# Joint attention stage: single key banks between other work on TensorE, that work one step later, a ring of three PSUM banks

## What is computed

```python
def _diff_combine(s, lam):
    p = jax.nn.softmax(s, axis=-1)
    B, _, Q, K = p.shape
    p = p.reshape(B, H_C, 2, Q, K)
    return p[:, :, 0] - lam * p[:, :, 1]

# prompt, for each block of 128 queries
s = jnp.einsum('bqhd,bkhd->bhqk', qi, k).astype(F32) * HD_C ** -0.5
s = jnp.where((kpos[None, :] <= qpos[:, None])[None, None], s, -jnp.inf)
a = _diff_combine(s, lam)
return jnp.einsum('bhqk,bkhe->bqhe', a, vf)

# samples
kp = cache_k[o][page_table].reshape(Bs, past, 2 * H_C, HD_C)
vp = cache_v[o][page_table].reshape(Bs, past, H_C, 2 * HD_C)
```

## Time and profile before

| | |
|---|---|
| median of three executions | 3101.52 us (3096.23 to 3102.09) |
| the profiled execution | 3103.92 us, its span 3101.8 us |
| busy share of the span: PE, DVE, ACT | 86%, 43%, 26% |
| the attention stage | from about 2013 to 2952 us of the span |
| DMA of the whole span | 535.76 MB |

### The profile page before, as it was taken

One profiled execution on the slowest core, in us unless ns is written; L12 is line 12 of the kernel. 1 busy time (PEld: TensorE's weight loads), 2 busy tenths in 40 slices (PEclk: granted clock), 3 DMA queues, 4 the chain that ended last, 5 costly groups with the idle time before them and its releaser, 6 DMA issues. The chain is left out here.

```text
span 3101.8 us, 45074 instructions
## 1 busy us (share of the span) xinstructions
PE 2677.2 (86%) x16187; PEld 1953.2 (63%) x16187; DVE 1345.8 (43%) x2285; ACT 797.2 (26%) x1981; POOL 392.1 (13%) x232
## 2 busy tenths in 40 slices
PE   4999999999929995899599999588888888888858
PEld 3988889888817774444277777455555555555546
DVE  3456553332234665122223433155555555555533
ACT  3122111111113331011111111144444444444421
POOL 3123322233000000000231311000000000000000
PEclk9999999999958998999899999799999999999979
DMA  3233321332146896521232331688898897897642
GB/s 108 79 95 98 100 79 58 112 105 80 55 108 185 274 287 193 197 82 44 66 96 90 112 95 53 197 303 278 318 337 283 312 336 276 322 341 278 242 144 93
DMA packets 323449, 535.76 MB, mean 173 GB/s; under 512 B 28525, under 2 KB 231810, under 8 KB 320042
## 3 DMA queue, kind: packets, MB, share of 16 engines
q1 hardware_dynamic: 320482, 524.66, 50.5%
q10 hardware_dynamic: 2792, 8.82, 0.8%
HBM read 432.06 MB, written 101.22 MB: 172 GB/s over the span
## 5 line engine op out<-in xcount | busy, mean ns | idle before, releaser
L2230 PE MATMUL at_ring<-ident,at_kp 128*128 128x128 f32 x2048 | 304.3, 287 | 126.6 <-DVE at_kT L2452 69.9
L2230 PEld LDWEIGHTS at_ring<-ident,at_kp 128*128 128x128 f32 x2048 | 230.8, 145 | 199.8 <-issue 145.2
L2452 DVE COPY at_kT<-at_ring 128x512 f32<-128x512 f32 x256 | 177.1, 692 | 182.1 <-PE at_ring L2230 168.4
L497 PE MATMUL p_col<-h_hi,p_wqk 128*128 128x352 f32 x768 | 248.7, 324 | 3.2 <-DVEq L675 3.2
L1884 PE MATMUL p_gm<-p_whl,h_hi 128*128 128x512 f32 (+1 forms) x576 | 229.9, 399 | 21.9 <-POOLq L1946 21.9
L499 PE MATMUL p_col<-h_hi,p_wqk 128*128 128x352 f32 x768 | 247.0, 322 | 0.0
L498 PE MATMUL p_col<-h_lo,p_wqk 128*128 128x352 f32 x768 | 246.9, 321 | 0.0
L1611 PE MATMUL oa_out<-oa_w,oa_yT 128*128 128x512 f32 x512 | 225.7, 598 | 9.0 <-ACT oa_yT L1667 5.4
L526 PE MATMUL p_row<-p_wvz,h_hi 128*128 128x512 f32 (+1 forms) x576 | 228.9, 397 | 3.6 <-ACT p_vst L600 3.6
L528 PE MATMUL p_row<-p_wvz,h_lo 128*128 128x512 f32 (+1 forms) x576 | 227.7, 395 | 0.0
L1886 PE MATMUL p_gm<-p_whl,h_lo 128*128 128x512 f32 (+1 forms) x576 | 227.7, 395 | 0.0
(11 more groups left out here) (341 smaller groups left out, 4431.4 us busy)
## 6 DMA issues: line engine op xcount, KB each, us to landing
at_kp<-in_cache_k SPq DMA_DIRECT2D x256, 512.0 KB, 4.7
at_vp<-in_cache_v SPq DMA_DIRECT2D x256, 512.0 KB, 5.7
p_wst<-in_w_in_a SPq DMA_DIRECT2D x64, 512.0 KB, 4.2
s_qk<-p_res SPq DMA_DIRECT2D x32, 528.0 KB, 2.8
mx_qk<-s_qk SPq DMA_DIRECT2D x16, 1024.0 KB, 10.6
p_wst<-in_w_in_c SPq DMA_DIRECT2D x64, 256.0 KB
s_v<-p_vst SPq DMA_DIRECT2D x64, 128.0 KB, 2.8
s_g<-p_gst SPq DMA_DIRECT2D x64, 128.0 KB, 2.7
```

The source lines that it names most:

```text
L497: pe.matmul(out[:, r, 0:TN], wx[:, 0, k, :], h_hi[:, k, at], start=k == 0, stop=False)
L2230: last = pe.transpose(bank("key", n, 2 * k + f)[:, h * PAGE:(h + 1) * PAGE], kp[:, n % 2, k, (4 * f + h) * P:(4 * f + h + 1) * P], c.ident[:])
L2452: dve.tensor_copy(kT[:, n % 2, 4:8, k * PAGE:(k + 1) * PAGE], bank("key", n, 2 * k + 1)[:].rearrange("p (h t) -> p h t", h=4)).then_inc(dv ...
```

## The change

Every piece stays, with the same shapes; three things are altered, all in `attend`.

1. The ring has three banks, and a fill waits for the use three places earlier. The bank `ov` is gone: the page values go through the ring as a ninth kind of use, taken by `add_page`.
2. PE's step is cut finer. `turn_keys` fills one bank, `page_scores` comes in two halves of four matmuls, and single key banks stand between the other pieces. The turned weights and the page scores of step s move to step s + 1, the rows to s + 2, the page values to s + 3, the pick one step later too; so the loop has one pass more (`LAST`).
3. ACT, DVE and SP follow. DVE's maximum is taken for each half apart (one more `tensor_reduce` and `tensor_scalar` a step, the elements the same), and ACT's two exponentials stand apart. SP issues the first key page of s + 2, then four value pages, then the other three key pages, and the store and the loads of a head in iteration 3 in place of 2.

The diff, cut to its core:

```diff
+    RING = 3
...
-        ring = [st.ps(f"ring{i}", [P, 512]) for i in range(2)]
+        ring = [st.ps(f"ring{i}", [P, 512]) for i in range(RING)]
         sc = st.ps("sc", [P, 2, T])
         ssc = st.ps("ssc", [P, 512])
-        ov = st.ps("ov", [P, 512])
...
-        LAST = NG + 3
+        LAST = NG + 4
...
+        def keys_at(s):
+            return s < NG
+
+        def weights_at(s):
+            return 1 <= s <= NG
+
+        def rows_at(s):
+            return 2 <= s <= NG + 1
+
+        def values_at(s):
+            return 3 <= s <= NG + 2
+
+        def pick_at(s):
+            return (s - 4) // NGB if s >= 4 and (s - 4) % NGB == NGB - 1 else None
+
         for s_ in range(LAST):
-            for k in range(GP):
-                if s_ < NG:
-                    use("key", s_, 2 * k, "act")
-                    use("key", s_, 2 * k + 1, "dve")
-                if k == 1 and 1 <= s_ <= NG:
+            for f in range(2 * GP):
+                if keys_at(s_):
+                    use("key", s_, f, ("act", "dve")[f % 2])
+                if f == 1 and values_at(s_):
+                    use("val", s_ - 3, 0, "dve")
+                if f == 2 and weights_at(s_):
+                    for i in range((tiles(s_ - 1) + 3) // 4):
+                        use("wgt", s_ - 1, i, ("act", "dve")[i])
+                if f == 4 and rows_at(s_):
+                    use("row", s_ - 2, 0, "act")
+                if f == 5 and weights_at(s_):
                     use("out", s_ - 1, 0, "act")
-                if k == 2 and 1 <= s_ <= NG:
-                    use("row", s_ - 1, 0, "act")
-            if s_ < NG:
-                for f in range((tiles(s_) + 3) // 4):
-                    use("wgt", s_, f, ("act", "dve")[f])
-            if s_ >= 2 and s_ - 2 < NG and (s_ - 1) % NGB == 0:
-                use("pick", (s_ - 1) // NGB - 1, 0, "act")
+            if pick_at(s_) is not None:
+                use("pick", pick_at(s_), 0, "act")
...
         def bank(kind, n, i):
-            return ring[fills[kind, n, i] % 2]
+            return ring[fills[kind, n, i] % RING]
 
         def wait_bank(pe, kind, n, i):
 
             u = fills[kind, n, i]
-            if u >= 2:
-                eng, count = uses[u - 2]
+            if u >= RING:
+                eng, count = uses[u - RING]
...
-                def keys(n):
-                    for k in range(GP):
-                        if n >= 2:
-                            sp.wait_ge(filled, fills["key", n - 2, 2 * k + 1] + 1)
-                        page(g["cache_k"], kp, k_loaded, n, k)
-
-                def values(n):
-                    for k in range(GP):
-                        if n >= 2:
-                            sp.wait_ge(v_used, GP * (n - 2) + k + 1)
-                        page(g["cache_v"], vp, v_loaded, n, k)
+                def key(n, k):
+                    if n >= 2:
+                        wait_fill(sp, "key", n - 2, 2 * k + 1)
+                    page(g["cache_k"], kp, k_loaded, n, k)
+
+                def value(n, k):
+                    if n >= 2 and k < GP - 1:
+                        sp.wait_ge(v_used, (GP - 1) * (n - 2) + k + 1)
+                    elif n >= 2:
+                        wait_fill(sp, "val", n - 2, 0)
+                    page(g["cache_v"], vp, v_loaded, n, k)
...
+                for s in range(NG + 1):
+                    if s + 2 < NG:
+                        key(s + 2, 0)
+                    if s >= 3:
+                        for k in range(GP):
+                            value(s - 1, k)
+                    if s + 2 < NG:
+                        for k in range(1, GP):
+                            key(s + 2, k)
+                    if s % NB == 3 and s >= NB:
+                        store(s // NB - 1)
+                        if s // NB + 1 < HC:
+                            head(s // NB + 1)
...
+                def turn_keys(n, f):
+                    k = f // 2
+                    if f % 2 == 0:
+                        pe.wait_ge(k_loaded[n % 2 * GP + k], 16 * (n // 2 + 1))
+                    wait_bank(pe, "key", n, f)
+                    for h in range(4):
+                        tile = (4 * (f % 2) + h) * P
+                        last = pe.transpose(bank("key", n, f)[:, h * PAGE:(h + 1) * PAGE], kp[:, n % 2, k, tile:tile + P], c.ident[:])
+                    last.then_inc(filled, 1)
...
+                    wait_bank(pe, "val", n, 0)
...
+                        last.then_inc(v_used if k < GP - 1 else filled, 1)
+
+                def page_scores(n, i):
+                    if i == 0:
+                        pe.wait_ge(act_took, took("key", n, 2 * GP - 2))
+                        pe.wait_ge(dve_took, took("key", n, 2 * GP - 1))
+                        if n >= 1:
+                            pe.wait_ge(p_ready, n)
+                    for j in range(JC):
+                        last = pe.matmul(ssc[32 * j:32 * j + 32, :], qz[:, n // NGB, j, i, :], kT[:, n % 2, j + JC * i, :],
+                                         start=i == 0, stop=i == 1)
+                    if i == 1:
+                        last.then_inc(s_ready, 1)
...
-                    if s < NG:
-                        turn_keys(s, 0)
-                    if 2 <= s <= NG + 1:
-                        page_values(s - 2)
-                    if s < NG:
-                        turn_keys(s, 1)
-                    if 1 <= s <= NG:
-                        sum_values(s - 1)
-                    if s < NG:
-                        turn_keys(s, 2)
-                    if 1 <= s <= NG:
-                        turn_rows(s - 1)
-                    if s < NG:
-                        turn_keys(s, 3)
-                        if s + 1 < NG:
-                            scores(s + 1)
-                        page_scores(s)
-                        turn_weights(s)
-                    if picks(s) is not None:
-                        pick(picks(s))
+                    for f in range(2 * GP):
+                        if keys_at(s):
+                            turn_keys(s, f)
+                        if f == 1 and values_at(s):
+                            page_values(s - 3)
+                        if f == 2 and weights_at(s):
+                            turn_weights(s - 1)
+                        if f == 3 and weights_at(s):
+                            page_scores(s - 1, 0)
+                        if f == 4 and weights_at(s):
+                            page_scores(s - 1, 1)
+                        if f == 4 and rows_at(s):
+                            turn_rows(s - 2)
+                        if f == 5 and weights_at(s):
+                            sum_values(s - 1)
+                    if s + 1 < NG:
+                        scores(s + 1)
+                    if pick_at(s) is not None:
+                        pick(pick_at(s))
...
-                def exps(s):
+                def exps(s, m):
                     n = tiles(s) * P
-                    act.wait_ge(max_ready, s + 1)
-                    for m in range(2):
-                        last = act.activation(pr[:, s % 2, m, 0:n], sc[:, m, 0:n], ACT.Exp, bias=o_mx[:, s % 2, m:m + 1], scale=SC,
-                                              accum_out=o_den[:, s % 2, m:m + 1])
-                    last.then_inc(sc_taken, 1)
+                    act.wait_ge(max_ready, 2 * s + m + 1)
+                    last = act.activation(pr[:, s % 2, m, 0:n], sc[:, m, 0:n], ACT.Exp, bias=o_mx[:, s % 2, m:m + 1], scale=SC,
+                                          accum_out=o_den[:, s % 2, m:m + 1])
+                    if m == 1:
+                        last.then_inc(sc_taken, 1)
...
+                    if rows_at(s):
+                        page_exps(s - 2)
+                    if keys_at(s):
+                        take_keys(s, 0)
+                        take_keys(s, 1)
+                    if weights_at(s):
                         take_weights(s - 1)
-                    if picks(s - 1) is not None:
-                        take_pick(picks(s - 1))
-                    if s < NG:
-                        take_keys(s, 0)
-                    if 1 <= s <= NG:
-                        page_exps(s - 1)
-                    if s < NG:
-                        take_keys(s, 1)
-                        exps(s)
-                    if 1 <= s <= NG:
+                    if keys_at(s):
+                        exps(s, 0)
+                        take_keys(s, 2)
+                    if rows_at(s):
+                        take_rows(s - 2)
+                    if keys_at(s):
+                        exps(s, 1)
+                    if weights_at(s):
...
-                    dve.wait_ge(v_used, GP * (n + 1))
+                    wait_fill(dve, "val", n, 0)
...
+                def maximum(s, m):
+                    top = o_mx[:, s % 2, m:m + 1]
+                    ch.link(dve.tensor_reduce(top, sc[:, m, 0:tiles(s) * P], AX_X, ALU.max))
```

(60 more changed lines are left out.)

51 lines of the change are left out of this document (10 added, 41 removed).

## The result

The changed kernel takes 2935.2 us (median of four, 2928.86 to 2948.84), the kernel before 3101.81 us in the same session: a ratio of 0.947, 95% interval 0.9435 to 0.951. The forecast was 2948, so the gain is 167 us where 154 were expected. The profiled execution took 2939.19 us, its span is 2937.1.

A forecast was written before the change was run, and what follows sets the result against it. PE was taken as the bound, idle in waits for free ring banks. Pace 88, stalls 5, changes of piece 2 and clock 1 make 96 us a head, 768 against 922.4: gain 154, median 2948 us, range 2915 to 3020.

The forecast's parts named there:

- PE's pace: In the attention stage, PE's unchanged matmuls and transposes take 88 us a head at full clock.
- The named stalls: PE's waits left at four places in the new order: 4.4 us, with 1 us of restarts about 5 a head.
- Tile count 8 into 1: PE waits 0.8 us for the page values' bank, behind ACT's rows and exponential and DVE's difference and key bank 7.
- Tile count 3: DVE's finish delays PE 1.2 us at the weights and 1.15 at the page values' bank: 2.35 us.
- The small ones at tile counts 2, 4, 7 and 8: Page values' bank 0.2 to 0.3 us late at 2 and 4; split maxima 0.1 to 0.2 at 7 and 8.
- The total idle time expected in the stage: A sign of being right: PE idle near 50 us in the attention stage, against 155.5 before.
- Changes of piece: PE's groups a step go from nine to thirteen, 0.06 us for each of four new ones: 2 us a head.
- The clock: PE's granted clock, 0.96 in the stage, rises to 0.99 or more; 4.7 us a head gained, 1 taken back.
- the rival built on it: Slower clock: all 36 transposes a step cost 0.124 us more, 132 us a head, 3236 us; slower clock's chance 0.05.
- The rival had them take over: DMA bounds the stage at 362 GB/s: period 97.5, about 100 us a head, time 2979 us; chance 0.20.
- The ring rival: New waits in the ring behind page values and DVE's strict list: 107 us a head, 3035 us; chance 0.17.
- The ends: Loop's end, last key bank to last copy (2936.9 to 2951.9 before), stays the same within 1 us despite one more pass.

The follow-up runs named there:

- the kernel with three edits: Changed kernel with key banks in pairs, the pick's stores issued by GpSimd and finish cut into four parts: 2900.58 us, 0.9359 of the kernel before.
- coarse form: Changed kernel with key banks in pairs again, three banks and the step's shift kept: 2926.68 us, then 2927.37 beside the changed kernel's 2929.58.

## Why the prediction was right, point by point

**PE's pace.** 88 us a head from starts in the earlier trace rows stands. The head from 2336.60 to 2432.18, in which the clock stays up, takes 95.58 us, of which PE is busy for 90.94; for pace, changes of piece and restarts 88 + 2 + 1 were set. The mean of six heads is 96.7, so falls of the clock cost 1.1, where 1 was set.

**The named stalls.** 4.4 us a head were placed, and the four listed waits come to 4.4 (30.8 us in seven heads), but the places do not all agree. Tile count 8 into 1: 0.8 set, 0.72 measured. Tile count 3: 2.35 set, 0.69 + 0.97 = 1.66 measured, at the two fills named. The small ones at tile counts 2, 4, 7 and 8 did not show; they were entered with 1.2 in all, though the bounds given for them make 0.6 to 1.0. And 2.0 us a head at tile count 5, ScalarE's issue of four DMAs, was missed: I followed what ACT computes and not what it issues, though the earlier trace rows end at the copy that precedes just these four. The kernel before issues the same four behind its pick, and PE then waited 1.19 us for the key bank that ACT copies next:

```profile
2152.55 2.88 ACTq L2380 DMA_DIRECT2D at_a<-at_oq  x4
2155.54 0.60 ACT L2331 ACTIVATE at_kT<-at_ring 128x512 f32<-128x512 f32 x1 [3.02 <-issue]
```

The sum of the stalls came out right by luck: the miss at tile count 5 covered what was set too high elsewhere. The total idle time expected in the stage, near 50 us, was above the prediction's own terms (5 us a head are 40) and above the 37.3 measured.

**Changes of piece.** 2 us a head; 1.1 of them (0.14 x 8) are seen at the page scores. The count behind it is off by one: a step of the kernel before has ten groups, not nine, so three are new and not four.

**The clock.** It went from 0.96 to 0.99, as set. The reason given, that no long stretch of transposes is left in the new order, is not what the runs show: the third bank alone keeps the old order and has 0.99 as well. The clock still falls in some heads, at places where PE waits. Two windows around the pick of one head, then the same two of the next:

```profile
2242.00:2245.00 3.00, 1.02 (x21) 0.40 (x14) 2.34 (x6) 1.45 (x4) 0.00 (x0) 1.00 1.04 380
2245.00:2248.00 3.00, 3.00 (x20) 1.98 (x20) 0.69 (x1) 1.97 (x4) 0.00 (x0) 0.58 1.06 405
...
2339.24:2342.24 3.00, 1.03 (x21) 0.41 (x14) 2.35 (x6) 1.45 (x4) 0.00 (x0) 1.00 1.04 380
2342.24:2345.24 3.00, 3.00 (x28) 1.82 (x32) 0.69 (x1) 1.86 (x4) 0.00 (x0) 1.00 1.07 415
```

Behind the wait of 1.98 us that ends at 2244.92 the granted clock was 0.58; behind the same wait one head later it was 1.00. So a wait stands before each of these falls but does not always bring one, and what else decides is not shown. A step holds 36 transposes besides the weights', as before, and in whole heads the clock stays at 1.00. So the rule in the Trainium skill (TensorE: Matmul & The Clock Gate, Part 4: PE-mode transpose), that the full clock does not engage for transposes, does not hold for this kernel; the rival built on it is refuted. Before the fall in the earlier trace rows PE had done only transposes with gaps, and so it had before the one at tile count 3, from the end of the page values at 2217.72 on (busy for 1.34 us from 2218 to 2221, then a clock of 0.60). Before the one at the pick it had done the page values, which are matmuls, and then nothing until 2244.92. What the three have in common is the idle time.

**The DMAs.** The rival had them take over at 362 GB/s. The stage moved 365 GB/s on average, the kernel with three edits 377 to 2759.83, and leaving out half of the loads gained nothing. One head of the kernel with three edits moved 396 GB/s at a share of 1.02. A step whose DMA share was 1.02 was no measure of the limit. The figure of some 358 GB/s on the HBM side (DMA: Bandwidth & Descriptors, Where 436 GB/s comes from, in the Trainium skill) was exceeded for the whole stage, with one core at work.

**The ring rival** set 107 us a head. It is what the third bank alone gives (105.7), without the shift. The changed kernel doesn't show it.

**The ends.** The last copy of ACT starts at 2786.67, the last key banks at 2770.90: 15.8 us, against 15.7 in the earlier trace rows.

## What to carry over

A wait for a free buffer is removed by two different things, a buffer more and a consumer that is asked a step later; each alone gave 85 and 34 us here (the second with the fine cut beside it), both together 167. A buffer covers a short lateness; to take away a long one, the work had to be asked for later. To forecast such a change, take each engine's pace from starts that follow without a gap, then walk the new order and set down every piece that stands ahead of a copy, DMA issues included. Finer pieces are worth trying in their coarse form too: here the coarse one was no slower, and with the leftover waits removed it was the faster. Before a few microseconds are given a cause, compare stretches in which the clock did not fall: such heads of the changed kernel took 95.4 to 95.7 us in both of its traces, and against them the 1.2 us a head of the fine cut could be seen, which the medians hid.

## What was not expected of the hardware

A DMA share of 0.97 was no bound on the time, with a page 6.3 us from issue to landing (4.6 before); at half of the loads it was 3.7 us and the time no shorter. And splitting eight 32x512 matmuls into two groups of four, with a key bank between, cost 0.14 us, while single key banks cost 0.43 to 0.59 us where 0.5 was the pace in pairs.
